# Two feed-forwards by seven products of quadrants (Strassen) in an fp32 kernel of one core

## The reference

```
def swiglu(u, w_gate, w_up, w_down):
    return (jax.nn.silu(u @ w_gate) * (u @ w_up)) @ w_down
...
mods = jnp.split(jax.nn.silu(c) @ w_ada[l] + b_ada[l], N_MOD, axis=-1)
u = modulate(rmsnorm(h, g_ff1[l]), sh1, sc1)
h = h + FFN_RES * gt1[:, None, :] * swiglu(u, w1_gate[l], w1_up[l], w1_down[l])
...   # attention and mLSTM branches
u = modulate(rmsnorm(h, g_ff2[l]), sh3, sc3)
h = h + FFN_RES * gt3[:, None, :] * swiglu(u, w2_gate[l], w2_up[l], w2_down[l])
```

## Time and profile before

| | us |
|---|---|
| median of 3 runs (lowest, highest) | 1227.39 (1226.31, 1228.52) |
| span of the profiled execution | 1226.5 |
| PE busy, PEld busy | 1215.9, 1056.1 |
| DVE, ACT, POOL busy | 500.7, 297.4, 80.4 |

### The profile page before, as it was taken

One profiled execution on the slowest core, in us unless ns is written; L12 is line 12 of the kernel. 1 busy time (PEld: TensorE's weight loads), 2 busy tenths in 40 slices (PEclk: granted clock), 3 DMA queues, 4 the chain that ended last, 5 costly groups with the idle time before them and its releaser, 6 DMA issues.

```text
span 1226.5 us, 17258 instructions
## 1 busy us (share of the span) xinstructions
PE 1215.9 (99%) x7122; PEld 1056.1 (86%) x7122; DVE 500.7 (41%) x1442; ACT 297.4 (24%) x855; POOL 80.4 (7%) x103
## 2 busy tenths in 40 slices
PE   9999999999999999999999999999999999999997
PEld 7888888996678888889988888898888998888887
DVE  4434440072027533351445442037765322157632
ACT  2110000042124434100300001034424421146542
POOL 0000000000012000011000000030000310000111
PEclk9999999999999999999999999999999999999999
DMA  9968873572475455566888885358242563543311
GB/s 347 336 236 295 308 248 124 205 275 95 151 234 155 174 206 197 183 236 223 278 307 309 309 290 187 105 203 280 78 122 80 187 215 112 153 122 104 104 70 35
DMA packets 163263, 241.52 MB, mean 197 GB/s; under 512 B 13057, under 2 KB 111551, under 8 KB 163184
## 3 DMA queue, kind: packets, MB, share of 16 engines
q1 hardware_dynamic: 155296, 230.45, 55.2%
q10 hardware_dynamic: 6784, 5.74, 1.6%
q0 software_dynamic: 1104, 4.22, 1.0%
HBM read 236.82 MB, written 4.62 MB: 197 GB/s over the span
## 4 chain that ended last, share of the span: by engine, by line
PE 95%; DVE 2%; ACT 1%; DMA 1%; POOL 0%; issue 0%; DVEq 0%; ACTq 0%
PE ps L189 93%; PE ps L192 2%; ACT U L195 1%; DVE tmpB L204 0%; DMA bias_row<-rows 0%; DMA arena<-bias_row 0%; DVE rstd L216 0%; ACT arena L195 0%; ACT tmpC L195 0%; DVE U L198 0%; POOL arena L198 0%; POOL tmpC L198 0%; DVE arena L216 0%; ACT rstd L195 0%; DVE arena L198 0%
## 5 line engine op out<-in xcount | busy, mean ns | idle before, releaser
L189 PE MATMUL ps<-U,slots 128*128 128x256 f32 (+2 forms) x3424 | 700.0, 365 | 0.2 <-DVE arena L198 0.2
L189 PEld LDWEIGHTS ps<-U,slots 128*128 128x128 f32 (+1 forms) x3424 | 601.4, 190 | 78.9 <-issue 5.0
L189 PE MATMUL ps<-arena,slots 128*128 128x256 f32 (+1 forms) x1840 | 324.1, 338 | 0.0
L189 PEld LDWEIGHTS ps<-arena,slots 128*128 128x128 f32 x1840 | 292.5, 191 | 30.1 <-issue 1.8
L207 DVE CUSTOM_DVE_ANT_0 slots<-slots,tmpA 128x1024 f32<-128x1024 f32 x104 | 123.2, 1230 | 5.1 <-DMA slots<-in_w_adaT 4.8
L195 ACT ACTIVATE tmpC<-ps 128x256 f32<-128x256 f32 (+3 forms) x95 | 38.4, 409 | 341.0 <-PE ps L189 334.8
L195 ACT ACTIVATE arena<-ps 128x512 f32<-128x512 f32 (+3 forms) x116 | 50.5, 459 | 153.2 <-PE ps L189 148.9
L204 DVE SCALAR_TENSOR_TENSOR tmpC<-tmpC,ps 128x256 f32<-128x256 f32 (+1 forms) x46 | 18.8, 409 | 149.3 <-ACT tmpC L195 149.3
L195 ACT ACTIVATE tmpC<-H 128x512 f32<-128x512 f32 (+2 forms) x32 | 15.8, 506 | 237.9 <-DVE H L204 195.8
L204 DVE SCALAR_TENSOR_TENSOR H<-ps,sm,H 128x256 f32<-128x256 f32 (+1 forms) x32 | 11.9, 413 | 136.9 <-PE ps L189 136.9
L195 ACT ACTIVATE arena<-arena,st 128x128 f32<-128x128 f32 (+2 forms) x128 | 48.5, 405 | 31.9 <-DVE st L201 31.9
(11 more groups left out here) (162 smaller groups left out, 747.4 us busy)
## 6 DMA issues: line engine op xcount, KB each, us to landing
slots<-in_w_adaT SPq DMA_DIRECT2D x14, 2048.0 KB, 7.8
slots<-in_w_in SPq DMA_DIRECT2D x14, 2048.0 KB, 9.2
slots<-in_w_down SPq DMA_DIRECT2D x16, 1408.0 KB, 6.6
...
```

The source lines that it names most:

```text
L189: return Nothing() if self.e is None else self.e.matmul(*a, **k)
```

## The change

The later blocks of gate/up (ff1: blocks 5 to 10, ff2: blocks 1 to 10) and three of the four pairs of down in each feed-forward are computed by seven products of quadrants in place of eight (Strassen's scheme in Winograd's form). The inner dimension, the pair of output tiles and the 256 tokens are each cut in two. So a block takes 7 products x 2 (gate, up) x 4 calls = 56 calls with 128 tokens in place of 32 calls with 256; a pair of down takes 7 x 11 = 77 calls with 128 tokens in place of 44 with 256.

The sums of quadrants are made so: of the activations once for each feed-forward on VectorE (`v_su`: four, 128x512; `v_sd`: four over 11 tiles, in two parts, 128x1152 and 128x256); of the weights for each block, t1 on VectorE and t2, t3, t4 on GpSimd (128x1024 each; 128x1408 for down). The partial sums of results are copied out of PSUM by ScalarE between the products (`s_gu`, `s_gu_rest`, `s_dn`) and put together by VectorE (`v_gu`: c1, c22; `v_gu_act`: silu times up for both tiles; `v_dn`). TensorE makes the products of a block in the order p1, p2, p6, p5, p7, p3, p4. The modulation weights no longer use the slots in the feed-forwards: they come as 512 KB pieces into a ring `AR` of four buffers in the arena, and `v_ada_chunks` handles up to four per block. `t_lambda` and `t_bias` both stand now ahead of block 5.

```diff
+        AR = ring(*[arena[:, 5632 + 1024 * i:6656 + 1024 * i] for i in range(4)])
+        for f, g0, counts in (("f1", 4, {4: 3, 5: 3, 6: 3, 7: 3, 8: 2, 9: 2}),
+                              ("f2", 18, {0: 3, 1: 4, 2: 3, 3: 3, 4: 3, 5: 3, 6: 3, 7: 3, 8: 3})):
...
+        def v_ada_chunks(e, chunks):
+            for g, c in chunks:
+                e.wait_ge(*s_achunk[AR.index(g, c)].at(g, c))
+                e.wait_ge(*dve.at("cr", 0 if g < 18 else 1, 1))
+                v_mod_column(e, AR.buf(g, c), mod_col(g) + c)
+                AR.close([dve.now()], g, c)
+                if c == 3:
+                    dve.mark("ada", g)
+                    e.wait_ge(*dve.now())
+                    v_ada_mods(e, g)
...
+        def v_su(e, f, tag):
...
+            e.tensor_tensor(SU[0], a21, a22, ALU.add).then_inc(*dve.up())
+            e.tensor_tensor(SU[2], a11, a21, ALU.subtract).then_inc(*dve.up())
+            e.wait_ge(*dve.now())
+            e.tensor_tensor(SU[1], SU[0], a11, ALU.subtract).then_inc(*dve.up())
+            e.wait_ge(*dve.now())
+            e.tensor_tensor(SU[3], a12, SU[1], ALU.subtract).then_inc(*dve.up("su", f))
+        def v_t1(e, f, b):
...
+            e.tensor_tensor(t[:, 0], w[:, :, 0:4, P:T], w[:, :, 0:4, 0:P], ALU.subtract).then_inc(*dve.up(f, "t1", b))
+        def p_t(e, f, b):
+            t, w = TG.buf(f, b), gu_block(f, b)
+            e.wait_ge(*dve.at(f, "t1", b))
+            e.wait_ge(*arrived(f + " gu", b))
+            e.tensor_tensor(t[:, 1], w[:, :, 4:8, P:T], t[:, 0], ALU.subtract).then_inc(*pool.up(f, "t2", b))
+            e.tensor_tensor(w[:, :, 0:4, P:T], w[:, :, 4:8, P:T], w[:, :, 0:4, P:T], ALU.subtract).then_inc(*pool.up(f, "t3", b))
+            e.wait_ge(*pool.at(f, "t2", b))
+            e.tensor_tensor(t[:, 2], w[:, :, 4:8, 0:P], t[:, 1], ALU.subtract).then_inc(*pool.up(f, "t4", b))
+        def t_gu(e, f, b):
...
+            i.then_inc(*pe.up(f, "p2", b))
+            e.wait_ge(*dve.at("su", f))
+            e.wait_ge(*pool.at(f, "t2", b))
+            e.wait_ge(*act.at(f, "s1", b))
+            for n in range(2):
+                i = product(A[:, n, 0:P], t[:, 1, n], SU[1], False)
+            i.then_inc(*pe.up(f, "p6", b))
...
+            e.wait_ge(*pool.at(f, "t3", b))
+            e.wait_ge(*act.at(f, "u2", b))
+            for n in range(2):
+                i = product(A[:, n, 0:P], w[:, n, 0:4, P:T], SU[2], False)
...
+            e.wait_ge(*pool.at(f, "t4", b))
+            e.wait_ge(*act.at(f, "u3", b))
...
+        def s_gu_rest(e, f, b, first=()):
...
+            if b - 1 >= (5 if f == "f1" else 1):
+                e.wait_ge(*dve.at(f, "c22", b - 1))
+            e.wait_ge(*pe.at(f, "p7", b))
+            e.activation(FG, A, ACT.Copy).then_inc(*act.up(f, "u3", b))
...
+        def v_gu(e, f, b):
...
+            e.wait_ge(*pe.at(f, "p3", b))
+            e.tensor_tensor(x_[:, 0].rearrange("p n j t -> p n (j t)"), C2[:, :, 0:T], E.rearrange("p n j t -> p n (j t)"), ALU.add).then_inc(*dve.up(f, "c1", b))
+            e.wait_ge(*act.at(f, "u3", b))
+            e.tensor_tensor(x_[:, 1, :, 1, :], x_[:, 1, :, 1, :], FG, ALU.add).then_inc(*dve.up(f, "c22", b))
+        def v_gu_act(e, f, b):
...
+            e.wait_ge(*act.at(f, "th", b))
+            e.stt(th, th, 1.0, x_[:, :, 0].rearrange("p h j t -> p h (j t)"), ALU.add, ALU.mult).then_inc(*dve.up())
+            e.wait_ge(*dve.now())
+            to = actT[:, 2 * b:2 * b + 2, :].rearrange("p j (h t) -> p h j t", h=2)
+            e.tensor_tensor(to, E, x_[:, :, 1], ALU.mult).then_inc(*dve.up())
...
+        def p_dn_t(e, f, p):
...
+            e.tensor_tensor(t2, hi[:, :, P:T], t1, ALU.subtract).then_inc(*pool.up(f + " dn", "t2", p))
+            e.tensor_tensor(lo[:, :, P:T], hi[:, :, P:T], lo[:, :, P:T], ALU.subtract).then_inc(*pool.up(f + " dn", "t3", p))
+            e.wait_ge(*(pe.at(f + " dn", "p6", p - 1) if p else pe.at(f, "p4", 10)))
+            e.wait_ge(*pool.at(f + " dn", "t2", p))
+            e.tensor_tensor(t4, hi[:, :, 0:P], t2, ALU.subtract).then_inc(*pool.up(f + " dn", "t4", p))
+        def t_dn(e, f, p):
...
+            product(A[:, 0:P], lo[:, :, 0:P], actT[:, 0:11, HALF[0]], True, 0).then_inc(*pe.up(n, "p1", p))
+            e.wait_ge(*arrived(n, 2 * p + 1))
+            product(C2[:, 0:P], hi[:, :, 0:P], actT[:, 11:22, HALF[0]], True, 11).then_inc(*pe.up(n, "p2", p))
+            e.wait_ge(*dve.at("sd", f))
+            e.wait_ge(*pool.at(n, "t2", p))
+            e.wait_ge(*act.at(n, "s1", p))
+            product(A[:, 0:P], t2, SD[:, 1], False).then_inc(*pe.up(n, "p6", p))
...
+        def v_gu_blocks(e, f, b0):
+            for b in range(b0, 11):
+                if b > b0:
+                    v_gu_act(e, f, b - 1)
+                chunks = CHUNKS[f].get(b, [])
+                v_ada_chunks(e, chunks[:2])
+                if b < 10:
+                    v_t1(e, f, b + 1)
+                else:
+                    v_sd(e, f, 0, 9)
+                    v_dn_t1(e, f, 0)
+                v_ada_chunks(e, chunks[2:])
+                v_gu(e, f, b)
+            v_gu_act(e, f, 10)
+            v_sd(e, f, 9, 11)
...
         def vector(e):
...
-            for half in range(2):
-                v_gate(e, "f2", 0, half)
-                v_gate(e, "f2", 1, half)
+            v_gate(e, "f2", 0, 0)
+            v_gate(e, "f2", 1, 0)
+            e.wait_ge(*pe.at("sums", "n3", 1))
+            v_t1(e, "f2", 1)
+            v_su(e, "f2", "n3")
+            v_gate(e, "f2", 0, 1)
+            v_gate(e, "f2", 1, 1)
             v_silu_c2(e)
...
-                s_gate(e, "f2", c)
+            s_gu_blocks(e, "f2", 1, [pool.at("mg", 3), dve.at("cr", 1, 1)])
```

More of the change, by code:

```diff
@@ new lines, in s_gu_tanh @@
+        def s_gu_tanh(e, f, b):
+            E, x_ = EG.buf(f, b), XG.buf(f, b)
+            th = E.rearrange("p h j t -> p h (j t)")
+            e.wait_ge(*dve.at(f, "c22", b))
+            e.wait_ge(*act.now())
+            e.activation(th, x_[:, :, 0].rearrange("p h j t -> p h (j t)"), ACT.Tanh, scale=0.5).then_inc(*act.up(f, "th", b))
+        def v_gu_act(e, f, b):
+            E, x_ = EG.buf(f, b), XG.buf(f, b)
+            th = E.rearrange("p h j t -> p h (j t)")
+            e.wait_ge(*act.at(f, "th", b))
[3 more added lines that the diff above has]
+            e.tensor_tensor(to, E, x_[:, :, 1], ALU.mult).then_inc(*dve.up())
+            dve.mark(f, "act", 2 * b)
+            dve.mark(f, "act", 2 * b + 1)
+            EG.close([dve.now()], f, b)
+            XG.close([dve.now()], f, b)
@@ new lines, in v_sd @@
+        def v_sd(e, f, k0, k1):
+            a11, a12, a21, a22 = (actT[:, 11 * k + k0:11 * k + k1, HALF[h]] for h in range(2) for k in range(2))
+            s1, s2, s3, s4 = (SD[:, n, k0:k1, :] for n in range(4))
+            e.wait_ge(*dve.at(f, "act", 10 + k1))
+            e.tensor_tensor(s1, a21, a22, ALU.add).then_inc(*dve.up())
+            e.tensor_tensor(s3, a11, a21, ALU.subtract).then_inc(*dve.up())
+            e.wait_ge(*dve.now())
+            e.tensor_tensor(s2, s1, a11, ALU.subtract).then_inc(*dve.up())
+            e.wait_ge(*dve.now())
+            e.tensor_tensor(s4, a12, s2, ALU.subtract).then_inc(*dve.up())
+            if k1 == 11:
+                dve.mark("sd", f)
@@ new lines, in t_dn, with product @@
+        def t_dn(e, f, p):
+            n = f + " dn"
+            (A, C2), free = QD.open(f, p)
+            for x in free:
+                e.wait_ge(*x)
+            lo, hi = dn_of(f, p)
+            t1, t2, t4 = (TD[(3 * p + i) % 4] for i in range(3))
+            def product(out, stationary, moving, start, c0=None):
+                for k in range(11):
+                    if c0 is not None:
+                        e.wait_ge(*dve.at(f, "act", c0 + k))
+                    i = e.matmul(out, stationary[:, k, :], moving[:, k, :], start=start and k == 0, stop=k == 10, skip_group_check=True)
+                return i
+            e.wait_ge(*arrived(n, 2 * p))
+            product(A[:, 0:P], lo[:, :, 0:P], actT[:, 0:11, HALF[0]], True, 0).then_inc(*pe.up(n, "p1", p))
[5 more added lines that the diff above has]
+            product(A[:, 0:P], t2, SD[:, 1], False).then_inc(*pe.up(n, "p6", p))
+            product(C2[:, P:T], t1, SD[:, 0], False).then_inc(*pe.up(n, "p5", p))
+            e.wait_ge(*pool.at(n, "t3", p))
+            e.wait_ge(*act.at(n, "u2", p))
+            product(A[:, 0:P], lo[:, :, P:T], SD[:, 2], False).then_inc(*pe.up(n, "p7", p))
+            W.close([pe.now()], n, 2 * p)
+            e.wait_ge(*act.at(n, "s5", p))
+            product(C2[:, P:T], hi[:, :, P:T], SD[:, 3], False).then_inc(*pe.up(n, "p3", p))
+            W.close([pe.now(), pool.at(n, "t4", p)], n, 2 * p + 1)
+            e.wait_ge(*pool.at(n, "t4", p))
+            e.wait_ge(*act.at(n, "u3", p))
+            product(A[:, 0:P], t4, actT[:, 11:22, HALF[1]], False).then_inc(*pe.up(n, "p4", p))
@@ L983, in t_bias @@
         def t_bias(e):
-            ps, free = X.open("bias")
```

(16 more changed lines are left out.)

289 lines of the change are left out of this document (232 added, 57 removed).

## The result

| | before | after |
|---|---|---|
| median, us (lowest, highest; 9 runs each) | 1227.46 (1226.22, 1228.52) | 1230.52 (1228.45, 1231.87) |
| span of the profiled execution, us | 1226.5 | 1229.5 |
| time after over time before, 95% interval | | 1.0023 (1.0013 to 1.0032) |

What follows compares the result with a forecast made beforehand. PE's work bounds the kernel, with VectorE and GpSimd taking turns at SBUF. 1226.5 - 32.3 + 32.9 stalls + 4.5 clock = 1231.6, with 0.9 for the median 1232.5, called 1232 us; range 1211 to 1249 (0.8).

Steps and rivals of the forecast that it cites:

- TensorE's own work, -32.3: Both feed-forwards: gate/up blocks 13.83 to 12.50 us, down pairs 19.02 to 17.19, saving 32.3 us in sum.
- GpSimd 2.34 alone for 1024, 3.15 for 1408: GpSimd weight sums, scaled from shorter rows: 2.34 and 3.15 us alone, 2.26 and 3.07 as a port turn.
- rival D: GpSimd sums: dearer through short runs and in-place writing; a third more gives 1262 us, a tenth 1242; chance 0.17.
- Block 5, 0.7: Block 5 of ff1: t2 late by 0.7 us because the bias row and its DMA on GpSimd come first.
- rival B: Shared port: VectorE's next instruction, following at once, goes ahead of a waiting GpSimd one; 1223.7 us; chance 0.18.
- Passages, 10.5 and 8.7: Block 10 to down: PE waits while VectorE and GpSimd take port turns, 10.5 us in ff1, 8.7 in ff2.
- VectorE ends silu and up of block 9 at 8 in ff1: Before down in ff1: VectorE finishes block 9 8 us after PE starts block 10, each operation having waited for GpSimd.
- Start of ff2, 7.6: Block 1 of ff2, ahead of p6: copy s1 waits for row CR, done at 611.3 us; stall 7.6 us.
- Middle blocks, 0.6 each: Three-piece gate/up blocks: port time 13.1 us against 12.50, lacking 0.6 each; stalls 3.3 us in ff1, 2.8 in ff2.
- The clock, 3 stretches of 1.5: After three PE pauses of 7 to 9 us the clock falls to half level, costing 1.5 us each, 4.5.
- the upper bound of 20: Clock loss after the pauses: at most half of 13 us each, 20 us in all.
- What was to show it: Profile signs: PE idle before down and in ff2's block 1, VectorE t1 or piece mean near 2, GpSimd over 3.

Runs made afterwards that it cites:

- the version held at the start of ff2: Changed kernel, but GpSimd's first t2 of ff2 waits until the row CR of the second c is done: 1228.65 us (one run).
- all three orders: Changed kernel with ff2's first t2 after CR, down's first t2 after block 10's silu and up, block 5's sums before the bias DMA: 1226.19 us, ratio 0.9989.

## Why the prediction was near, and which of its steps were off

The forecast was 1232 and slower; 1230.5 was measured. Its mechanism, that both engines take turns while both operands lie in SBUF, was right: the versions without GpSimd's sums, with them on VectorE and with one more bear it out from three sides. Step by step:

- **TensorE's own work, -32.3.** Right: 12.50 us a block and 111.6 ns a record. By medians the version on VectorE is 31 us faster than the kernel before (ratio 0.9748), 1.3 short of this term. (The two profiled executions differ by 34.0, but that of the version on VectorE was the fastest of its five, 2.0 under their median.) That the weight loads set the pace with 128 tokens is not shown: in the earlier trace rows the matmuls are busy 4.00 of 4.00 as well, and no run parts the two.
- **GpSimd 2.34 alone for 1024, 3.15 for 1408; 2.26 and 3.07 as a turn.** The shortest of 1024 is 2.34, at the passage t2 takes 3.17. In a middle block the turns are about 2.2. Right, and rival D falls: strided reads and writing in place cost nothing that shows.
- **Block 5, 0.7 (in the 3.3 for ff1).** 4.1 measured: the largest miss. I had GpSimd take its turn after one piece, as in the earlier trace rows; there VectorE kept its place through three pieces. That is the behaviour of rival B, shown at this one place only: in the version held at the start of ff2, each of three such pieces waits for one sum (3.36 us each).
- **Passages, 10.5 and 8.7.** Right in place and cause, but 6.6 and 7.3. The step that failed is "VectorE ends silu and up of block 9 at 8 in ff1": 4.6 was measured, and in ff2 5.3 (729.55 - 724.20) in place of 6.2. In ff1 it follows from the step before. In the version with a stop between the pieces, where block 5 pauses for 0.5 (0.7 was forecast), block 9 ends at 8.0, and the passage costs 180.13 - 171.43 + 1.26 = 10.0. The prediction's 10.5 is itself 0.5 more than its own times give: "up" at 25.7, four sums of 0.42, and "sd" wanted at 17.4 make 10.0.
- **Start of ff2, 7.6.** 6.9, released by ScalarE's s1 behind `CR`, as described.
- **Middle blocks, 0.6 each, 3.3 - 0.7 + 2.8 = 5.4 in all.** 0 as pauses. The lack exists and is smaller: t1 follows t1 every (709.26 - 632.61) / 6 = 12.78 us, against PE's 12.51, so 0.27 a block in place of 0.6. In ff2 t2 of block 2 is ready 4.6 us ahead of its p6 (623.15 and 627.72), and that lead, which the pause and the slow clock behind it gave (I had counted 2.4), has shrunk to 1.8 in block 7 (688.47 and 690.25), never to 0. Without the lead it shows as 12.78 a block (all three orders), and in ff1, in the version with a stop between the pieces, p6 of block 10 comes 158.03 - 93.90 = 64.1 us behind p6 of block 5, 1.6 more than five times 12.51 (2.6 of the 3.3 were forecast for that). The rows of the changed kernel: t1, t2, c22, t3, and t1 of the next block:

```profile
683.90 1.22 DVE L198 TENSOR_TENSOR arena<-slots 128x1024 f32<-128x1024 f32 x1
...
685.20 3.27 POOL L198 TENSOR_TENSOR arena<-slots,arena 128x1024 f32<-128x1024 f32 x1 [4.25 <-DVE arena L198]
...
686.78 1.97 DVE L198 TENSOR_TENSOR tmps<-tmps,rstd 128x256 f32<-128x256 f32 x1
688.42 2.54 POOL L198 TENSOR_TENSOR slots<-slots 128x1024 f32<-128x1024 f32 x1
...
696.67 1.23 DVE L198 TENSOR_TENSOR arena<-slots 128x1024 f32<-128x1024 f32 x1
```

- **The clock, 3 stretches of 1.5, 4.5 in all.** 4 stretches of 2.25 to 2.57, 9.8 in all. This term was too small by half, and its ground is not shown: the prediction read the slow records of the earlier trace rows as the 1.2 GHz level and then the full pace, but the granted clock is 1.00 there and over the whole of the first 30 us. Whether the clock made those records slow (24 in 9.02 to 14.08, 211 ns each) stays open, and with it the upper bound of 20. A window of PE in the kernel before, with the clock in the third place from the end:

```profile
10.00:14.00 4.00, 4.00 (x22) 1.00 1.06 393
```

The Trainium skill (TensorE: Matmul & The Clock Gate, section What's actually happening) describes a clock that is held down by default and released by activity; the trace agrees behind all four pauses of the changed kernel, with 0.50 for some 5 us behind each, while at the program's start it records no half level.

- **What was to show it.** The pauses are where the prediction put them, but two signs came out smaller: GpSimd's sums of 1024 have a mean of 2.8 us (over 3 was named), and t1 and the pieces one of 1.35 and 1.30 (near 2). The waiting fell on c22, silu and up instead, with means of 2.04, 1.69 and 1.55 for 0.41 to 0.69 alone.
- **Two slips that change nothing here.** At 342 us the GpSimd addition was not nearly over but had 0.63 of its 1.28 us left; 0.63 and two VectorE additions of 0.64 make the 1.91, so the reading of turns stands. Rival D's own terms (2.2 for 15 blocks and 5) make 38 and not 30, 1270 and not 1262.

Pauses 32.9 were forecast and 24.9 measured, clock 4.5 and 9.8: 37.4 and 34.7. That the sum came out within 2 us is in part luck: two errors, 8.0 too much pause and 5.3 too little clock, went against each other, and so did the miss at block 5 and the shorter passage that it brought. What remains open is why GpSimd was kept out through three pieces in block 5 and let in between two at 540 us and in the version held at the start of ff2. There the operations are the same as in block 5; at 540 us GpSimd's is one of 512 elements. It is shown, by one run each, that neither taking away the DMA ahead of t2 nor asking 0.8 us earlier changes it, and that a stop of VectorE does.
